# Recurrence gates with two contraction tiles: the neighbours' rows in one mixed tile

## What is computed

```python
proj = h @ w_in                       # h = RMSNorm(x); u and y are two slices of proj, each 1280 wide
u = causal_conv(u, conv_w, width 4) + conv_b
ub = u.reshape(B, S, 16, 80)
r = sigmoid(einsum("bsnc,ncd->bsnd", ub, w_rg).reshape(B, S, 1280) + b_rg)
i = sigmoid(einsum("bsnc,ncd->bsnd", ub, w_ig).reshape(B, S, 1280) + b_ig)
log_a = -8 * r * softplus(-lru_lambda)
a = exp(log_a)
b = sqrt(-expm1(2 * log_a)) * (i * u)
h_t = a_t * h_(t-1) + b_t             # scan over the sequence
lru_out = h * gelu(y)
```

## Time and profile before

| | us |
|---|---|
| time, median of 3 runs (1734.5 to 1734.67) | 1734.54 |
| the profiled execution's own time | 1732.49 |
| its span in the profile | 1730.7 |
| recurrent stage and gates of the first half, in the span | about 44 to 206 |
| the same of the second half | about 525 to 685 |

### The profile page before, as it was taken

One profiled execution on the slowest core, in us unless ns is written; L12 is line 12 of the kernel. 1 busy time (PEld: TensorE's weight loads), 2 busy tenths in 40 slices (PEclk: granted clock), 3 DMA queues, 4 the chain that ended last, 5 costly groups with the idle time before them and its releaser, 6 DMA issues.

```text
span 1730.7 us, 26755 instructions
## 1 busy us (share of the span) xinstructions
PE 1692.4 (98%) x7676; PEld 1392.5 (80%) x7676; DVE 801.4 (46%) x878; ACT 561.0 (32%) x1034; POOL 1320.2 (76%) x1344
## 2 busy tenths in 40 slices
PE   8999999999999999999999999999999999999995
PEld 6787888888888878888888888888888888888884
DVE  5899736651277987766421733211611232111013
ACT  4577435442236765254422322111200211111000
POOL 5799966777788999777777877776777777666774
PEclk8999999999999999999999999999999999999997
DMA  4333332232343333422323434322433343224331
GB/s 142 102 88 89 116 98 85 79 98 94 108 128 106 90 89 108 155 75 76 96 94 103 140 130 143 109 96 93 137 100 95 111 143 132 94 95 141 96 97 60
DMA packets 111228, 183.15 MB, mean 106 GB/s; under 512 B 12352, under 2 KB 38208, under 8 KB 111168
## 3 DMA queue, kind: packets, MB, share of 16 engines
q1 hardware_dynamic: 97056, 156.15, 29.2%
q10 hardware_dynamic: 14112, 26.22, 4.5%
HBM read 173.94 MB, written 8.39 MB: 105 GB/s over the span
## 4 chain that ended last, share of the span: by engine, by line
PE 86%; issue 5%; POOL 4%; DVE 3%; ACT 1%; DMA 0%; POOLq 0%; ACTq 0%; SPq 0%; DVEq 0%
PE ps L426 27%; PE ps L425 26%; PE ps L424 26%; POOL w_hi L358 3%; POOL w_lo L361 1%; PE ps L486 1%; PE ps L565 1%; PE ps L487 1%; PE ps L488 1%; PE ps L555 0%; PE ps L557 0%; PE ps L556 0%; PE ps L580 0%; PE ps L579 0%; DVE rows L1482 0%
## 5 line engine op out<-in xcount | busy, mean ns | idle before, releaser
L361 POOL TENSOR_TENSOR w_lo<-w_raw,w_hi 128x512 fp32r<-128x512 f32 (+2 forms) x664 | 849.4, 1279 | 55.4
L358 POOL TENSOR_SCALAR w_hi<-w_raw 128x512 fp32r<-128x512 f32 (+2 forms) x664 | 466.5, 703 | 334.2 <-PE ps L426 261.1
L424 PE MATMUL ps<-h_hi,w_hi 128*128 128x512 f32 x1376 | 538.1, 391 | 9.9 <-POOL w_lo L361 7.5
L426 PE MATMUL ps<-h_hi,w_lo 128*128 128x512 f32 x1376 | 541.0, 393 | 0.0
L425 PE MATMUL ps<-h_lo,w_hi 128*128 128x512 f32 x1376 | 538.8, 392 | 0.0
L424 PEld LDWEIGHTS ps<-h_hi,w_hi 128*128 128x128 f32 x1376 | 258.4, 188 | 71.2 <-issue 6.4
L425 PEld LDWEIGHTS ps<-h_lo,w_hi 128*128 128x128 f32 x1376 | 258.4, 188 | 57.3
L426 PEld LDWEIGHTS ps<-h_hi,w_lo 128*128 128x128 f32 x1376 | 258.6, 188 | 54.3
L1122 DVE TENSOR_TENSOR acc<-acc,sq 128x512 f32<-128x512 f32 x55 | 66.3, 1206 | 226.7 <-ACT sq L969 201.7
L1447 DVE TENSOR_TENSOR tmp<-ps,tmp 128x512 f32<-128x512 f32 x44 | 30.4, 691 | 301.8 <-PE ps L426 301.8
L426 PE MATMUL ps<-f_hi,w_lo 128*128 128x512 f32 x352 | 138.7, 394 | 0.0
(11 more groups left out here) (193 smaller groups left out, 2431.3 us busy)
## 6 DMA issues: line engine op xcount, KB each, us to landing
w_raw<-w_f SPq DMA_DIRECT2D x176, 256.0 KB, 3.0
w_raw<-w_step SPq DMA_DIRECT2D x64, 256.0 KB, 2.6
w_raw<-w_b SPq DMA_DIRECT2D x64, 256.0 KB, 3.0
w_raw<-w_d SPq DMA_DIRECT2D x64, 256.0 KB, 2.7
w_raw<-w_a SPq DMA_DIRECT2D x96, 128.0 KB, 2.0
xs<-x_t ACTq DMA_DIRECT2D x32, 256.0 KB, 3.4
w_raw<-w_q SPq DMA_DIRECT2D x32, 256.0 KB, 3.2
w_raw<-w_o SPq DMA_DIRECT2D x32, 256.0 KB, 3.0
```

Source lines behind the costliest of these rows:

```text
L358: nc.gpsimd.tensor_scalar(w_hi[:, s, w], w_raw[:, s, w], 1.0, 0.0, ALU.mult, ALU.add).then_inc(w_hi_made, 1)
L361: nc.gpsimd.tensor_tensor(w_lo[:, s, w], w_raw[:, s, w], rd(w_hi[:, s, w]), ALU.subtract).then_inc(w_lo_made, 1)
L424: mm(out, w_hi[:, s, w], x_hi, start=(k == 0), stop=False)
L426: last = mm(out, w_lo[:, s, w], x_hi, start=False, stop=(k == total - 1))
```

## The change

The blocks of 80 have a property that the change uses: for j = 1, 2, 3, 6, 7, 8 (MIXED) the rows needed of the tile behind lie within its partitions 0 to 63 and those of the tile before within its partitions 64 to 127. So both neighbours' rows fit in one tile of 128 partitions. A gate then has two contraction tiles: its own and the mixed one. Tile 5 needs only its own and the one behind it and goes from three to two as well. That makes 20 per gate, 40 for both gates of a half, where there were 54.

- Three mixed tiles in turn, `mix_hi` and `mix_lo`, lie in the space of `v_hl`, which is not in use then.
- Once `uc_hi` of tile j is made, ACT copies its partitions 0 to 63 to the mixed tile of j-1 and its partitions 64 to 127 to that of j+1, where those are in MIXED: 12 copies of 64x512 in a half. DVE does the same for `uc_lo`.
- On ACT the copies stand behind `decay(j-2)` and ahead of `gelu(j)`; on DVE behind `recurrence(j-2)`, at the end of the step.
- The gates of a mixed tile wait for both copies of both parts, ahead of their first matmul.
- The weights of a mixed tile in DRAM are unchanged; three transfers bring two tiles of them (two of 64x128, one of 128x128) where one of 128x384 brought three. POOL splits 256 columns, not 384.
- The loops over the steps' weight blocks in SP and POOL are written out.

The core of the diff; the two lists of transfers and of POOL's waits follow the same pattern:

```diff
+MIXED = (1, 2, 3, 6, 7, 8)
...
+        mix_hi = at("mix_hi", [P, 3, T], F32R, reg_v + 4 * KV_HEADS * 2 * HD)
+        mix_lo = at("mix_lo", [P, 3, T], F32R, reg_v + 4 * (KV_HEADS * 2 * HD + 3 * T))
...
+                    elif i in MIXED:
+                        sp_eng.dma_start(w_raw[0:P // 2, s, P:2 * P],
+                                         dram[g, 0:P // 2, off + 2 * P:off + 3 * P]).then_inc(mix_loaded[s], 16)
+                        sp_eng.dma_start(w_raw[P // 2:P, s, P:2 * P],
+                                         dram[g, P // 2:P, off:off + P]).then_inc(mix_loaded[s], 16)
+                        sp_eng.dma_start(w_raw[:, s, 0:P], dram[g, :, off + P:off + 2 * P])\
+                            .then_inc(w_loaded[s], 16)
...
+            def gates(h, j, n, slot):
                 J = j + KR * h
-                last_tile = size == 2 and first is None
-                pe.wait_ge(uc_lo_made, J + (1 if last_tile else 2))
+                pe.wait_ge(uc_lo_made, J + (1 if j == KR - 1 else 2))
...
-                tiles = first or [(q + d) % 4 for d in (-1, 0, 1)][:size]
+                if j in MIXED:
+                    pe.wait_ge(mix_hi_made[j % 3], 2 * (2 * h + 1 + (j > 5)))
+                    pe.wait_ge(mix_lo_made[j % 3], 2 * (2 * h + 1 + (j > 5)))
...
 ACT, step j:
                     gate_root(h, j - 2)
                     decay(h, j - 2)
+                    mix(h, j)
                     gelu(h, j, n + 6, j % 4)
...
 DVE:
+            def mix(h, j):
+                dve.wait_ge(uc_lo_made, j + KR * h + 1)
+                for to, r in ((j - 1, slice(0, P // 2)), (j + 1, slice(P // 2, P))):
+                    if to in MIXED:
+                        nc.vector.tensor_copy(mix_lo[r, to % 3, :], rd(uc_lo[r, j % 4, :]))\
+                            .then_inc(mix_lo_made[to % 3], 1)
...
                     conv_lo(h, j, j % 4)
                     recurrence(h, j - 2, (j - 2) % 4)
+                    mix(h, j)
```

More of the change, by code:

```diff
@@ L69 @@
 V_BLOCKS = [4, 4, 4, 4]
+MIXED = (1, 2, 3, 6, 7, 8)
+GATED = {"step": 0, "tail": 8}
 A_STEP = [2, 2, 2, 2] + [3, 3, 2, 2]
@@ L214, in build @@
         w_loaded = [sem(f"w_loaded{i}") for i in range(RING)]
+        mix_loaded = [sem(f"mix_loaded{i}") for i in range(RING)]
+        mix_hi_made = [sem(f"mix_hi_made{i}") for i in range(3)]
+        mix_lo_made = [sem(f"mix_lo_made{i}") for i in range(3)]
         par_loaded = sem("par_loaded")
@@ L316, in load, with load_gates @@
                     off += size * P
+            def load_gates(dram, g, sizes, n, i0):
+                off, i, half = 0, i0, slice(0, P // 2)
+                for b, size in enumerate(sizes):
+                    s = b % RING
+                    wait_pos(sp_eng, w_lo_made, n + b - RING + 1)
+                    if size == 4:
+                        sp_eng.dma_start(w_raw[:, s, 0:CAP], dram[g, :, off:off + CAP])\
+                            .then_inc(w_loaded[s], 16)
[5 more added lines that the diff above has]
+                        sp_eng.dma_start(w_raw[:, s, 0:P], dram[g, :, off + P:off + 2 * P])\
+                            .then_inc(w_loaded[s], 16)
+                    else:
+                        at0 = off + (size - 2) * P
+                        sp_eng.dma_start(w_raw[:, s, 0:2 * P], dram[g, :, at0:at0 + 2 * P])\
+                            .then_inc(w_loaded[s], 16)
+                    off += size * P
+                    i += size < 4 and sizes[b - 1] < 4
             def stream(stages, bases):
@@ L323, in stream @@
                     first = 1 if base == 0 else 0
+                    if name in GATED:
+                        for g in range(groups):
+                            load_gates(dram, g, sizes, base + g * len(sizes), GATED[name] + 4 * g)
+                        continue
                     if first:
@@ L369, in stream @@
                     first = 1 if base == 0 else 0
+                    if name in GATED:
+                        for g in range(groups):
+                            split_gates(sizes, base + g * len(sizes), GATED[name] + 4 * g)
+                        continue
                     assert base % RING == 0 and len(sizes2) % RING == 0
@@ L454, in stat_sum @@
                 mm(ps[:, BK_STAT, :], ones_r[:], acc_lo[:], start=False, stop=True).then_inc(stat_mm, 1)
-            def gates(h, j, n, size, slot, q, first=None):
+            def gates(h, j, n, slot):
                 J = j + KR * h
-                last_tile = size == 2 and first is None
-                pe.wait_ge(uc_lo_made, J + (1 if last_tile else 2))
-                if last_tile:
+                pe.wait_ge(uc_lo_made, J + (1 if j == KR - 1 else 2))
+                if j == KR - 1:
                     pe.wait_ge(r_made, J)
                     pe.wait_ge(i_made, J)
-                tiles = first or [(q + d) % 4 for d in (-1, 0, 1)][:size]
+                if j in MIXED:
+                    pe.wait_ge(mix_hi_made[j % 3], 2 * (2 * h + 1 + (j > 5)))
+                    pe.wait_ge(mix_lo_made[j % 3], 2 * (2 * h + 1 + (j > 5)))
+                tiles = [(j + d) % 4 for d in ((0, 1) if j in (0, 5) else (-1, 0))]
                 for g in range(2):
-                    project(4 + g, n + g, slot + g, [size], uc_hi, uc_lo, tiles=tiles)
+                    s, out = (slot + g) % RING, ps[:, 4 + g, :]
+                    pe.wait_ge(w_lo_made, n + g + 1)
+                    for k in range(2):
+                        if j not in MIXED:
+                            x_hi, x_lo = uc_hi[:, tiles[k], :], uc_lo[:, tiles[k], :]
+                        elif k == 0:
+                            x_hi, x_lo = uc_hi[:, j % 4, :], uc_lo[:, j % 4, :]
+                        else:
+                            x_hi, x_lo = mix_hi[:, j % 3, :], mix_lo[:, j % 3, :]
+                        w = slice(k * P, (k + 1) * P)
+                        mm(out, w_hi[:, s, w], x_hi, start=(k == 0), stop=False)
+                        mm(out, w_hi[:, s, w], x_lo, start=False, stop=False)
+                        last = mm(out, w_lo[:, s, w], x_hi, start=False, stop=(k == 1))
+                    last.then_inc(blocks_done, 1)
             def head(h, j, ready):
@@ L500, in recurrent @@
                     project(0, n, slot, UNIT, h_hi, h_lo)
[L501 to L505, removed]
+                    gates(h, j - 2, n + 2, slot + 2)
                     wait_pos(pe, gelu_made, j + KR * h)
@@ L513, in kvq @@
                 project(BK_K[0], n, 0, UNIT, h_hi, h_lo)
-                gates(h, 8, n + 2, 3, 2, 0)
+                gates(h, 8, n + 2, 2)
                 pe.wait_ge(u_copied, 2 * KR * (h + 1))
                 project(BK_K[1], n + 4, 0, UNIT, h_hi, h_lo)
-                gates(h, 9, n + 6, 2, 2, 1)
+                gates(h, 9, n + 6, 2)
                 pe.wait_ge(gelu_made, KR * (h + 1))
```

22 lines of the change are left out of this document (added).

## The result

The changed kernel takes 1766.07 us, the median of five runs (1765.08 to 1767.22), against 1734.54 for the kernel before (1731.98 to 1736.47, five runs): a ratio of 1.0184, 95% interval [1.0172, 1.0196]. It is slower by 31.5 us.

A forecast was written before the change was run, and what follows sets the result against it. PE, DVE and POOL were taken to run in step, with PE busy 98%; the change closes a 17.0 us loop. Loops 24.7, tiles 4, 5 and 9 1.5, head 1.2, clock 4.8 give +32.2, so 1766 us; range 1746 to 1788.

The forecast's parts named there:

- The forecast case: The loop through PE, ACT and DVE holds at mixed tiles and slows the kernel to 1766 us; 82%.
- The closed loop: At each mixed tile: DVE copy 0.60, PE gates 3.04, ACT gate functions 6.79, DVE recurrence 6.6; 17.0 us together.
- The high end of the range: Mixed-tile loops of 18.2 us, with a copy of 0.9 and DVE's part 7.43: +39 plus other terms, about 1784.
- The twelve loops: Recurrences at the 12 mixed tiles: 179.3 us before, 204.0 after, +24.7 us.
- The clock: Half TensorE clock at the first mixed gates of each half: 2.4 us each, 4.8 in all, bounds 0 and about 29.
- the prediction's own last sign: The prediction called itself wrong if the granted clock is 0.50 after most stops.
- The rival of the clock falling at every stop: The loop holds and every mixed gate product runs at 1.2 GHz: +56 us, 1791; 8%.
- PE's stops: PE idle ahead of each mixed gate's first matmul, 3.3 us each, 12 times, released by DVE's low copy.
- The smaller terms: Tiles 4, 5 and 9 +1.5 us (bounds 0 and 4); copies in the head 0.6 per half, 1.2; weight transfers nothing.
- The sum: Whole kernel: 24.7 + 1.5 + 1.2 + 4.8 = +32.2 us, 1764.7 on the profiled scale, 1766.7 on the median's.
- The rule on the shared ports: DVE and POOL share ports, the loser blocks; DVE's part shortest whenever POOL has filled its ring, low end 15.7 a loop.
- The copy comes in time, 1715: Rival: DVE's recurrence ends before PE wants the gates; up to 19.2 us come off, about 1715; 6%.

The follow-up runs named there:

- The useless matmuls: Changed kernel plus matmuls into an unread bank ahead of each wait for a mixed tile (20 at tile 1, 18 at tile 6, 9 elsewhere): 1751.49 us.
- the all-on-ACT kernel: Changed kernel with all 48 copies on ACT, between the sqrt and the wait for decay, and none on DVE: 1720.01 us.
- ACT's copies late: Changed kernel with DVE's copies moved ahead of the recurrence, ACT's left behind decay: 1730.32 us.

## Why the prediction was right

**The forecast case is what happened**: 1766 forecast, 1766.07 measured. The closed loop is what the experiments show; that the number met is luck, since terms that were off by 2 to 12 us cancelled. By steps, on the scale of the profiled executions:

- *The closed loop.* Shown. In the loops at full clock the pieces were forecast 0.60, 3.04, 6.79, 6.6 and measured 1.02, 3.12, 6.68, 6.10: 17.0 against 16.92. Two errors cancel here. The 0.60 was right for a copy while POOL rests: 0.58 and 0.59 were measured where it did. But the premise that POOL would rest then held for 2 of the 12 copies; the other ten met a POOL instruction. DVE's part was 0.5 shorter than the forecast; the row that came nearest was the shortest one, 5.59. Over all twelve, against the forecast's own terms, copy and hand-over cost 13.2 us (7.2), PE 53.6 (36.5 and 4.8 for the clock), ACT 79.1 (81.5), DVE 69.7 (79.2). The high end of the range took 0.9 for the copy, less than ten of the twelve measured ones.
- *The twelve loops.* They were to be 204.0 us and were 215.7 against 179.5 before, +36.2 where +24.7 was forecast, and 4.8 for the clock beside it. Four of them (16.92, 16.92, 16.91, 17.01) are the forecast's; the other eight hold all of the 12 us above it. The step that was mis-sized most is the clock's.
- *The clock.* The price of one restart was right: 2.4 forecast, 5.56 - 3.12 = 2.44 measured at 192.56; three of the eight cost only 1.4 to 1.6. The count was wrong: two forecast, eight happened. PE's pieces beyond 3.12 add up to 16.2 us against 4.8. That is also why PE is busy for only 2.6 us less than before, with 19.2 us of matmuls gone. The eight loops are only 12.6 us over 16.92 each, mainly since DVE's piece was 5.4 to 5.5 us and not 6.1 in seven of them. By the prediction's own last sign, the clock at 0.50 after most stops, this term was wrong. The earlier trace rows showed a stop of 2.49 us that did nothing, and I let the forecast stop of 3.3 us pass as much the same. It isn't: no stop of 3.57 or more kept the clock. The useless matmuls show it causally, 14.6 us back for 148 matmuls more. The rival of the clock falling at every stop (8%) came true at eight of twelve.
- *Why eight stops and not two.* The first mixed gates of a run of three, to which PE comes with a lead, stop it longest, and that happens at tile 6 (6.39 and 4.51 us), behind the tiles without a mixed one, as well as at tile 1 (6.99 and 5.21). The stop behind a loop with slow gates was 2.03 to 2.23 in all six cases, the one behind a loop at full clock 3.59 and 3.57. The slow gates themselves don't shorten it, since they lengthen the loop by as much as they lengthen PE's work: from 91.73 to 109.54 PE works for 17.81 - 2.23 = 15.58, from 174.98 to 192.56 for 17.58 - 3.59 = 13.99, and the 1.59 between them is in the gates of the first (4.71 against 3.12). The stops differ by 1.36, which is DVE's piece (5.41 against 6.11) and the next copy with its hand-over (1.01 against 1.67): which POOL instruction DVE meets. That slow gates shift POOL's work so is argued, not tested.
- *PE's stops.* 3.3 us each forecast; 43.1 / 12 = 3.6 measured, but spread from 2.03 to 6.99.
- *The smaller terms.* Steps 4, 5 and 9 were to cost +1.5 and gave 1.2 back. The head was to cost 1.2 and cost 0.9. Behind the recurrent stages the lateness passed on whole, as said: `q_lo` ends 19.4 us later in the first half and PE stands 1.66 us ahead of it; at the second it is 35.9 us in all.
- *The sum.* 36.2 - 1.2 + 0.9 = 35.9, and the rest of the kernel gave 1.2 back: +34.7. The forecast was +32.2 on this scale; it met the median to 0.1 us because the profiled execution is 1.15 us over the median where the one before was 2.05 under it. By that, and by the terms above, the exact agreement is luck. The sum itself gave 1766.7, rounded down. The range held with 20 us on either side.
- *The rule on the shared ports.* By the Trainium skill, SBUF — State Buffer, section on the two separate sides, an instruction that finds the shared ports taken blocks until the other engine's instruction ends. The trace agrees: the copies of 0.83 and 1.49 us ended 0.27 or 0.28 behind the POOL instruction that ran when they started, and those that met none took 0.41. What failed is the premise that POOL would have filled its ring and rest: it was at work again at ten of the twelve copies.
- *The rivals.* "The copy comes in time, 1715" was rightly refused for this order of the queues, and is what the all-on-ACT kernel is: 1720.01. The 5 us between the two go with PE's new waits, 6.7 us, of which 3.8 are for POOL and 2.1 for the one mixed gate at 68.10.

## What to carry to other kernels

When a cheap copy is put between two engines, draw the loop that its place in the in-order queue closes: what stands ahead of it there, and whether that work waits for the result which the copy feeds. While such a loop over three engines sets the pace, only PE's work inside it counts (148 useless matmuls in the stops cost nothing), and the idle time which it leaves is paid a second time if the clock falls; once the loop is open, the copy still belongs on the engine that has room (here ACT, 10 us better than early on DVE, 1720.0 against 1730.3, and 46 better than behind DVE's recurrence). And when a forecast meets to the microsecond, check its terms one by one: here they were off both ways.

## What was not expected of the hardware

- The lower clock also holds while PE is fully busy after a stop: 5.00 us busy with 12 matmuls at 0.50, in 605 to 610. Stops of 2.03 to 2.23 us fell on either side (four kept the clock, two lost it), and with ACT's copies late two stops of 2.71 us did too: in the 5.00 us behind the one that ended at 147.89 the granted clock was 0.66, behind the one that ended at 624.38 it was 1.00. So the length of the one stop doesn't settle it.
- A copy of 64 partitions took ACT 0.622 us, with hardly any spread (613 to 632 ns), and its casts of 128 partitions in the same stage take the same (614 to 636 ns). DVE's 64x512 copy spread from 410 to 1493 ns in one kernel, by the POOL instruction that it met, though alone it is the faster one. An engine without a spread is the safer home for work on a tight path.
